# A two-model block on one core: both attentions worked two heads at a time, and ScalarE centring the retention's values

## The reference, cut to what matters

```
s = einsum('bhnid,bhnjd->bhnij', qc, kc) * intra_decay
o = einsum('bhnij,bhnjd->bhnid', s, vc) + cross-chunk part
mu = mean(o, -1); o = (o - mu) * rsqrt(var + eps)
outs: win_sum / count - x, one window width for each 64 of the 256 pool channels
```

```
even, 256 context queries: softmax(q k_c / 8) v_c                     # 256 keys
even, 256 latent queries:  softmax([q k / 8 + bias, q k_c / 8]) [v, v_c]   # 512 keys
odd, 256 latent queries:   softmax(q k / sqrt(96)) v                  # 512 keys, 16 heads
```

## Time and profile before

| | |
|---|---|
| time, three runs | 2205.44, 2209.46, 2211.41 us, median 2209.46 us |
| the profiled execution's own time | 2207.22 us |
| its span in the trace | 2205.4 us, so 1.8 us lie around it |
| busy: PE, PEld | 2142.4 us (97%), 1958.4 us (89%) |
| busy: DVE, ACT, POOL | 1590.7 us (72%), 1062.0 us (48%), 164.4 us (7%) |
| mean granted clock of TensorE | 0.994 of full |
| read from HBM | 331.61 MB, 151 GB/s over the span |

### The profile page before, as it was taken

The page is one execution under the profiler, slowest core; times in us unless marked ns, Lnnn a source line. Parts: engine busy times, 40 slices in busy tenths (PEclk is TensorE's granted clock), DMA queues, the critical chain, the costliest instruction groups (busy, mean ns, idle before and its releaser), DMA issues. The chain is left out here.

```text
span 2205.4 us, 35256 instructions
## 1 busy us (share of the span) xinstructions
PE 2142.4 (97%) x14758; PEld 1958.4 (89%) x14758; DVE 1590.7 (72%) x2423; ACT 1062.0 (48%) x1546; POOL 164.4 (7%) x198
## 2 busy tenths in 40 slices
PE   9999999999999999999999989999999999999997
PEld 8999989999999998999897776998888877689997
DVE  6878998878988798998842676566555346758774
ACT  6443646443543554644552446445444225746653
POOL 1201102201200100200100010000000002000000
PEclk9999999999999999999999999999999999999999
DMA  6665526666566543777331120123222222013552
GB/s 268 233 237 193 208 91 232 246 232 255 210 231 246 197 154 115 273 272 251 121 119 53 58 100 15 46 79 114 96 96 96 96 96 77 20 62 130 176 187 96
DMA packets 48335, 334.94 MB, mean 152 GB/s; under 512 B 5612, under 2 KB 6716, under 8 KB 8880
## 3 DMA queue, kind: packets, MB, share of 16 engines
q1 hardware_dynamic: 38384, 267.47, 34.1%
q0 software_dynamic: 9792, 65.21, 7.8%
HBM read 331.61 MB, written 1.05 MB: 151 GB/s over the span
## 5 line engine op out<-in xcount | busy, mean ns | idle before, releaser
L2020 DVE TENSOR_TENSOR WLO<-RAW,WHI 128x2048 fp32r<-128x2048 f32 x252 | 576.4, 2292 | 212.3 <-ACT WHI L1453 209.4
L461 PE MATMUL PS<-XB,WHI 128*128 128x256 f32 (+1 forms) x3072 | 697.0, 322 | 8.3 <-DVE XB L2391 4.0
L1453 ACT CAST WHI<-RAW 128x2048 fp32r<-128x2048 f32 x252 | 476.5, 1894 | 283.6 <-DMA RAW<-in_dn_c 79.2
L461 PEld LDWEIGHTS PS<-XB,WHI 128*128 128x128 f32 x3072 | 513.7, 191 | 55.7 <-issue 11.3
L461 PE MATMUL PS<-XHI,WHI 128*128 128x272 f32 (+1 forms) x1760 | 498.9, 290 | 5.9 <-ACT XHI L1461 5.8
L461 PE MATMUL PS<-XB,WLO 128*128 128x256 f32 (+1 forms) x1536 | 491.9, 320 | 0.0
L461 PE MATMUL PS<-XHI,WLO 128*128 128x272 f32 (+1 forms) x1760 | 490.0, 288 | 0.0
L461 PE MATMUL PS<-XLO,WHI 128*128 128x272 f32 (+1 forms) x1760 | 481.7, 287 | 2.3 <-DVE XLO L2066 2.3
L461 PEld LDWEIGHTS PS<-XHI,WHI 128*128 128x128 f32 x1760 | 329.2, 189 | 9.8 <-issue 8.8
L461 PEld LDWEIGHTS PS<-XHI,WLO 128*128 128x128 f32 x1760 | 326.3, 189 | 0.0
L461 PEld LDWEIGHTS PS<-XLO,WHI 128*128 128x128 f32 x1760 | 322.6, 189 | 4.1 <-DVE XLO L2066 3.6
(11 more groups left out here) (367 smaller groups left out, 2633.3 us busy)
## 6 DMA issues: line engine op xcount, KB each, us to landing
AW<-in_ada POOLq DMA_DIRECT2D x48, 1024.0 KB, 7.1
RAW<-in_up_c SPq DMA_DIRECT2D x44, 1024.0 KB, 4.9
RAW<-in_up_a SPq DMA_DIRECT2D x42, 1024.0 KB, 5.0
RAW<-in_up_b SPq DMA_DIRECT2D x42, 1024.0 KB, 5.1
RAW<-in_mix SPq DMA_DIRECT2D x30, 1024.0 KB, 4.9
RAW<-in_dn_a SPq DMA_DIRECT2D x22, 1024.0 KB, 4.9
RAW<-in_dn_b SPq DMA_DIRECT2D x22, 1024.0 KB, 5.0
RAW<-in_dn_c SPq DMA_DIRECT2D x22, 1024.0 KB, 4.9
```

The lines of the kernel that those rows point to most:

```text
L461: return pe.matmul(o, w, x, start=first, stop=last)
L1453: act.copy(WHI1[:, s, 0:w], RAW[:, s, 0:w]).then_inc(w1_high, 1)
L2020: v.tensor_tensor(WLO1[:, s, 0:w], RAW[:, s, 0:w], WHI1[:, s, 0:w].bitcast(F32), ALU.subtract)\
```

## The change

- Items become pairs: heads 2i and 2i+1 with the same 128 queries are one step, 16 in each layer. Both heads' scores, maxima, exponentials, transposes and copies are issued one after the other; one `place_high` and one `place` write all 128 rows.
- In the even layer QZ is gone. Each head's scores contract over its own 64 rows of G (rows 0 to 63 and 64 to 127) into its own bank. PE waits for `na_taken` in place of GpSimd's step, and GpSimd's memset and two copies are gone.
- The values' stationary operand is 64 columns wide, and the two heads' products of one key block are written to rows 0 to 63 and 64 to 127 of one bank, alternating head by head.
- A pair's scores wait for both exponentials of the pair that last used its banks. With banks (2, 3) that is the pair just ahead, with banks (0, 1, 2, 3) the pair before that.
- `between(2p)` and `between(2p + 1)`, the head norm's pieces, both stand at the end of pair p's step.
- The retention's values are centred by ScalarE, right behind `copy_values`: two small scalings and six additions of a bias.
- The two widest pool sums are made for the second half of the pool channels alone.

```diff
-        def na_item(h, t):
-            ...
-            return item((QZ[:, h, t * P:(t + 1) * P], G[:, 12 + h // 2, 0:keys]), keys, NAD ** -0.5,
-                        lambda j: VN[:, j, h // 2 * P:h // 2 * P + P], q,
+        def na_pair(i, t):
             keys = CTX if t < 2 else L2
             c = slice(P * (t % 2), P * (t % 2) + P)
+            return {"qk": [(G[side_of(e), 16 + i, t * P:(t + 1) * P], G[side_of(e), 12 + i, 0:keys]) for e in range(2)],
+                    "keys": keys, "scale": NAD ** -0.5, "v": lambda j, e: VN[:, j, (2 * i + e) * 64:(2 * i + e) * 64 + 64],
+                    "out": [XB[:, t // 2, n, i, c] for n in range(2)],
...
@@ GpSimd
-            pool.memset(QZ[:, :, :], 0.0).then_inc(pool2_step, 1)
-            pool.wait_ge(na_taken, 8)
...
@@ TensorE, attend
+                at_once = len(banks) // 2
+                def scores(p):
+                    it = pairs[p]
+                    if p >= at_once:
+                        pe.wait_ge(at_max, 2 * (base + p - at_once) + 2)
+                        pe.wait_ge(at_exp, 2 * (base + p - at_once) + 2)
+                    outs = [PS[:, banks[(2 * p + e) % len(banks)], :] for e in range(2)]
+                    for e, (a, b) in enumerate(it["qk"]):
+                        last = mm(pe, outs[e][:, 0:it["keys"]], a, b, True, it["bias"] is None)
...
+                        for e in range(2):
+                            mm(pe, outs[e][:, CTX:L2], IDN8[:, :], it["bias"][e], False, True).then_inc(at_scores, 1)
...
+                def values(p):
...
                     for j in range(nk):
-                        last = mm(pe, PS[:, 6 + n % 2, 0:P], it["v"](j), turned[n % 2][:, j, :], j == 0, j == nk - 1)
+                        for e in range(2):
+                            last = mm(pe, PS[side_of(e), 6 + b % 2, 0:P], it["v"](j, e), turned[e][:, j, :], j == 0,
+                                      j == nk - 1)
...
+                scores(0)
+                for p in range(len(pairs)):
+                    if p + 1 < len(pairs):
+                        scores(p + 1)
+                    turn(p)
+                    if p >= 1:
+                        values(p - 1)
+                    between(2 * p)
+                    between(2 * p + 1)
@@ ScalarE, copy_values
+                    act.wait_ge(v_copied, 2 * l + z + 1)
+                    act.activation(VS[:, z, 0:2, :], VS[:, z, 0:2, :], ACT.Identity, scale=-1.0 / P)
+                    act.activation(VS[0:META, z, 2, :], VS[0:META, z, 2, :], ACT.Identity, scale=-1.0 / P)\
+                        .then_inc(v_mean, 1)
+                    act.wait_ge(v_mean, 2 * l + z + 1)
+                    for t in range(3):
+                        w = P if t < 2 else META
+                        for h in range(2):
+                            o = V1[0:w, t, 256 * z + P * h:256 * z + P * h + P]
+                            last = act.activation(o, o, ACT.Identity, bias=VS[0:w, z, t, h:h + 1])
@@ ScalarE, softmax
+                for p in range(len(pairs)):
+                    weights(p)
+                    if p >= 1:
+                        copy_turned(p - 1)
+                    if p >= 2:
+                        place_high(p - 2)
...
@@ VectorE, mixer
-                centre_values(0)
...
-                        st.link(v.tensor_tensor(PT_[j][:, :, lo:n], src[:, :, lo:n], src[:, :, lo - w:n - w], ALU.add))
+                        t = slice(0, 2) if j < 2 else slice(1, 2)
+                        st.link(v.tensor_tensor(PT_[j][:, t, lo:n], src[:, t, lo:n], src[:, t, lo - w:n - w], ALU.add))
@@ VectorE, attend
+                top(0)
+                for p in range(len(pairs)):
+                    norm(p)
+                    if p + 1 < len(pairs):
+                        top(p + 1)
+                    if p >= 2:
+                        place(p - 2)
+                    between(2 * p)
+                    between(2 * p + 1)
```

More of the change, by code:

```diff
@@ L1226, in even_output @@
+                values(len(pairs) - 1)
             def even_output():
-                pe.wait_ge(at_out, len(EVEN_ITEMS))
+                pe.wait_ge(at_out, len(EVEN_PAIRS))
                 pe.wait_ge(head_step, HEAD_LOW[3])
@@ L2605, in place @@
                     v.wait_ge(at_high, b + 1)
[L2606 to L2607 removed]
+                    hi, lo = pairs[p]["out"]
+                    v.tensor_tensor(lo, PS[:, 6 + b % 2, 0:P], hi.bitcast(F32), ALU.subtract).then_inc(at_out, 1)
                 top(0)
[L2610 to L2617 removed]
@@ L2618, in attend @@
-                for n in range(len(items) - 2, len(items)):
-                    place(n)
+                for p in range(len(pairs)):
[4 more added lines that the diff above has]
+                        place(p - 2)
+                    between(2 * p)
+                    between(2 * p + 1)
+                for p in range(len(pairs) - 2, len(pairs)):
+                    place(p)
             def even_output():
```

215 lines of the change are left out of this document (82 added, 133 removed).

## The result

The changed kernel takes 2193.89 us, the median of 4 runs (2191.74 to 2194.91); the kernel before 2209.15 beside it (2205.44 to 2211.41). The ratio is 0.9931, 95% interval 0.9914 to 0.9948. The profiled execution took 2194.37 us, its span 2192.5.

The account below looks back on a forecast made before the run. PE bounds the odd attention and the even one with 512 keys, handovers with 256; the mixers lose PE waits and half clock. 2207.2 - 10.4 - 7.4 + 2.3 = 2191.7, with 2.24 for the median 2193.9 us; range 2184 to 2203.

Parts of the forecast that it names:

- Retention's values: First network's two mixers: PE's wait shrinks to about 0.2 us and the clock stays up, -10.4 us, bounds -5 and -11.
- Rival B: Mixers give little, because ScalarE's instructions delay a rounding or another wait leaves the clock low: 2199.4 us, chance 0.12.
- Odd attention: Two heads' value products run side by side, pair period 3.86 us against 4.38: -7.4 us, bounds -13.3 and +6.8.
- rival A: Both attentions: the two heads' values overlap little or not, 2212.9 us, no measurable change; chance 0.10.
- mild form: Overlap of the two heads' values only by the skill's ratio: odd stage gives 4 us, kernel 2199.
- Even attention: Even stage in pairs: ring gains -6.0, against fill +2.7, head norm +4.8, clock +0.8; sum +2.3 us, bounds -6 and +9.
- Rhythm: Even attention, one pair at a time round the ring: 4.65 us against 5.24, 2.8 against 2.94; -6.0 us.
- Fill: Even attention's start: first `place` two steps in, a step now 2.8 us, not an item's 1.47; +2.7 us.
- Head norm: Seven even pair steps carry its pieces, a 512-wide VectorE operation of 0.69 us lying bare in each: +4.8 us.
- the one stretch at even odds: Even attention: half clock at the table loads' hole of almost 4 us costs up to 1.7 us; at even odds 0.8.
- Rivals C and D: Even attention: C, clock stays at half level, 2225 us, chance 0.04; D, head norm's pieces hide, 2185.7 us, chance 0.12.
- GpSimd's memset and copies: Removed work and the wait on `na_taken`: they end well ahead of the attention's first product, so 0 us.

Follow-up runs that it names:

- e2: The kernel before with only the odd attention in pairs, retention and even attention as before; 2197.38 us, ratio to before 0.995 to 0.998.
- e1: The kernel before with only the retention's part of the change, both attentions as before; 2199.09 us, ratio to before 0.995 to 0.998.
- e3: The changed kernel with its even attention put back, one head at a time with GpSimd's padded queries; 2191.43 us, ratio to before 0.991 to 0.994.
- e9: The changed kernel with the head norm behind the even attention and four score banks in place of two; 2181.50 us, ratio to before 0.986 to 0.990.
- e11: e3 with the head norm's pieces worked behind the even attention in place of between its items; 2196.42 us, ratio to before 0.994 to 0.997.
- e6: The changed kernel with the odd attention's values over 128 stationary columns per head, pairs kept, no overlap; 2202.32 us, ratio to before 0.997 to 0.999.
- e5: The changed kernel with GpSimd's memset and two query copies put back, read by nothing; 2196.37 us, ratio to before 0.994 to 0.997.
- e8: The changed kernel with the head norm's pieces worked behind the last even pair, two score banks kept; 2192.15 us, ratio to before 0.991 to 0.995.
- e10: The changed kernel with filler products of ones on PE ahead of the even attention's scores; 2201.56 us, ratio to before 0.997 to 0.999.
- e12: e9 with filler products of ones on PE in the idle times of the head norm's chain; 2184.03 us, ratio to before 0.987 to 0.991.

## Why the prediction was right, and what in it was not

The total was met (2193.9 forecast, 2193.89 measured), but to the last digit it was luck, twice over. Between the two profiled executions the span shrank by 12.9 us where the sum had 15.5: GpSimd's work gave 2.4 us more than forecast, and the even attention, the place at 548 us and the odd attention gave 1.9, 2.6 and 0.7 us less. Then the median was taken to lie 2.24 us above the profiled execution, as before the change; it lay 0.5 below, and that closed the gap.

*Retention's values, -10.4.* The first half held: the wait shrank to 0.23 us (forecast 0.2) in both layers, 2 x 2.8 us. The second half, that each wait is paid once more in the clock, held for the one profile of before that the forecast was read from: there the two mixers gave 5.7 + 4.5 = 10.2. It isn't a fixed price of the wait: in e2 both waits stand and the clock stays up, and the mixers' part on top of e2 is worth 6.0 us. Behind them, "the loads must keep up" decided. From the first mixer to the second the changed kernel takes 2.6 us longer than before, e1 4.6, e3 2.2, e9 0.5 and e11 nothing, with the same instructions up to there; e2, with the mixers of before, takes 1.1 longer. The largest single wait in that part, the one at 548 us, goes with when the loads land. Rival B named another wait and a low clock as what could spoil the gain, and both appeared in this execution, though the change did not bring them.

*Odd attention, -7.4.* Held: -6.7 in the profile, -8.25 in executions without the half clock at its start. (The way out of the column groups went into the sum as 0.11 us where its own working gives 3.57 less 3.44, 0.13; it changes 0.3 us in all.) The values of the pair after the one shown start 3.81 us behind its own (1913.04 against 1909.23), with 3.86 forecast, and e6 shows that the overlap is the whole of it; rival A fell. Its mild form, an estimate from the ratio of the Trainium skill (TensorE: Matmul & The Clock Gate, Part 3: Packing small matmuls), would be 4 us; the runs show 8.25 for two tiles of 64 columns.

*Even attention, +2.3.* Measured +4.2 in the changed kernel's profile, +3.4 in e5's and +2.5 in e6's, by three terms that were each mis-sized. Rhythm: 4.42 and 2.58 us per pair where I had 4.65 and 2.8, against 5.24 and 2.94, so -9.4 in place of -6.0. Fill: the first `place` stands 9.7 us in with pairs at full clock (e6) and 6.1 with items (e11), so +3.7 in place of +2.7, and up to +5.1 with the clock down there (e5, e8). Head norm: 19.8 to 21.3 us between pairs against 11.9 between items, +7.9 to +9.4 in place of +4.8, clock included. I had counted one VectorE operation lying bare per step; the rows show a mean product, two centrings and a square in series ahead of the exponentials. The hole at the logarithm came as drawn, 3.66 us on PE and 4.30 on VectorE:

```profile
1341.70 0.69 ACT L1845 ACTIVATE HSTD<-PS,EPS 128x512 f32<-128x512 f32 x1 [2.87 <-PE PS L460]
1342.41 1.28 ACT L1862 ACT_TABLE_LOAD   x1
...
1344.51 0.16 DVE L2598 RECIPROCAL STAT<-STAT 128x1 f32<-128x1 f32 x1 [4.30 <-ACT PR L1862]
...
1345.30 2.08 PE L460 MATMUL PS<-G 64*128 64x512 f32 x4 [3.66 <-ACT PR L1862]
```

The mean clock of the stage fell to 0.90 (0.94 in e6), more than the one stretch at even odds. At the start it cost 0.75 us for each 3.4 us at half level; what it cost further on stays open, since e10 did not separate it. Rivals C and D fell.

*GpSimd's memset and copies, 0.* This step failed: -2.4. I asked only when they end and who waits for them, not whom they hold up while they run. Their removal is the one gain of the even attention's edit that no other term took back; with that work put back the kernel is at 2196.37 us (e5), but the intervals of the two ratios overlap (0.994 to 0.997 against 0.991 to 0.995), so the 2.4 us are read from the cells and not from the total.

## What to carry to other kernels

A stage in which a pair fills all its PSUM banks runs at the pace of one pair's round trip, and every foreign piece between the pairs becomes a link of that trip; two more banks, with the foreign work put behind, turned a stage that had lost 2.5 to 4.2 us into a gain of some 11 us over the changed kernel here. The foreign work put behind did nothing by itself (e8). Before pricing removed work at nothing, look at what the neighbours of that engine last beside it and without it. Before pricing a fall of the clock from one profile, look at a second execution: the stretches read here as the price of a wait were absent in the next one with the same wait. And where a total comes out exact, check the parts: here the place behind the mixers, the even attention's rhythm, its head norm and GpSimd's work were each off by 2 us or more.

## What the runs showed of the hardware

Two products of 64 stationary columns in different column groups start 6 or 7 ns apart and take the time of one: the next two start 102 or 103 ns behind them, once 153. Three float32 operations of VectorE on SBUF stood still for nearly the whole rest of a GpSimd memset or copy (0.49 us became 2.23, 0.62 became 2.13, 2.29 became 3.98). Loads of 1 MB that were issued at the same place landed 4.9 to 7.6 us later, the next ones 4.9 to 9.3 us later, from one execution to another. Stretches of 3.4 us at half clock come and go between executions of the same instructions: behind waits of PE of 1.9 to 3.1 us (at 305, 548, 1083, 1880 us), and near 1185 us behind sixteen products four columns wide that took 1.94 us, with no wait. The same waits stand in executions where the clock stays up. One stretch was worth 1.3 to 1.6 us in the mixers and the cells, where PE binds, and nothing that could be measured in e12, so differences of 2 us between single profiles say little.
